# A 14-stage transformer chain in one kernel: inverse roots by logarithm and exponential, squares and an update on GpSimd, and fillers on TensorE between the stages

## The reference

```python
# first block, per sublayer (swiglu, stick-breaking attention or gated recurrence)
h = rmsnorm(x, g) * (1 + scale) + shift
x = x + [0.5 *] (1 + gate) * sublayer(h)
# between the blocks
x = rmsnorm(x, final_norm_g)
# second block, per sublayer (latent attention, convolution, pooling or squared-ReLU MLP)
h = rmsnorm(x, norm_g[i, 0 or 2]) * (1 + scale) + shift
x = x + gate * rmsnorm(sublayer(h), norm_g[i, 1 or 3])
```

## Time and profile before

| what | value |
|---|---|
| timed runs | 2570.82, 2563.72 and 2575.38 us; median 2570.82 us |
| profiled execution, own time | 2580.46 us |
| its span in the profile | 2578.8 us |
| TensorE busy / VectorE / ScalarE / GpSimd | 2358.3 / 1666.9 / 1199.6 / 334.9 us |
| TensorE's mean granted clock | 0.927 of full speed |

### The profile page before, as it was taken

How to read it: one execution, slowest core, us unless ns; L and a number is a source line. 1 busy time by engine, 2 the same in 40 slices (tenths; PEclk the granted TensorE clock), 3 DMA queues, 4 the chain that set the end, 5 groups by cost and what they waited for, 6 DMA issues and landing times.

```text
span 2578.8 us, 43638 instructions
## 1 busy us (share of the span) xinstructions
PE 2358.3 (91%) x17650; PEld 2262.1 (88%) x17650; DVE 1666.9 (65%) x1960; ACT 1199.6 (47%) x1761; POOL 334.9 (13%) x481
## 2 busy tenths in 40 slices
PE   3999999999999958999879999998997899888997
PEld 2999978999999957999848998888996899867997
DVE  6667655667767665767765766855766675654653
ACT  1444445543544464544534543435544554554543
POOL 0111000111111021211000214300201120000210
PEclk6999989999999988999869998998998999888999
DMA  8689763779688723878443775403784477222552
GB/s 309 233 283 315 254 233 102 269 269 326 241 299 293 251 82 124 307 263 296 158 164 104 250 272 183 131 3 121 253 275 133 139 255 249 82 98 66 181 191 70
DMA packets 292525, 523.88 MB, mean 203 GB/s; under 512 B 9318, under 2 KB 184849, under 8 KB 292369
## 3 DMA queue, kind: packets, MB, share of 16 engines
q1 hardware_dynamic: 262417, 358.07, 41.8%
q0 software_dynamic: 29952, 163.59, 17.8%
HBM read 520.57 MB, written 1.05 MB: 202 GB/s over the span
## 4 chain that ended last, share of the span: by engine, by line
PE 87%; DVE 7%; ACT 3%; issue 2%; POOL 0%; ACTq 0%; DVEq 0%; POOLq 0%
PE bk L1210 11%; PE bk L1211 11%; PE bk L1212 11%; PE bk L1118 10%; PE bk L1119 10%; PE bk L1120 10%; PE bk L1261 4%; PE bk L1171 3%; PE bk L1452 2%; PE bk L1191 1%; PE bk L1192 1%; PE bk L1193 1%; DVE inv L1623 1%; DVE mod_acc L1596 1%; PE bk L1316 1%
## 5 line engine op out<-in xcount | busy, mean ns | idle before, releaser
L1577 DVE TENSOR_TENSOR w_lo<-raw,w_hi 128x1024 fp32r<-128x1024 f32 (+5 forms) x720 | 834.2, 1185 | 611.2 <-ACT w_hi L721 609.2
L721 ACT ACTIVATE w_hi<-raw 128x1024 fp32r<-128x1024 f32 (+5 forms) x720 | 684.4, 977 | 737.2 <-PE bk L1120 402.8
L1210 PE MATMUL bk<-a_hi,w_hi 128*128 128x256 f32 x2336 | 668.5, 286 | 4.4 <-DVE a_lo L1643 4.4
L1211 PE MATMUL bk<-a_lo,w_hi 128*128 128x256 f32 x2336 | 667.1, 286 | 0.0
L1212 PE MATMUL bk<-a_hi,w_lo 128*128 128x256 f32 x2336 | 666.7, 285 | 0.0
L1118 PE MATMUL bk<-hid_hi,w_hi 128*128 128x256 f32 x1664 | 465.7, 280 | 0.0
L1120 PE MATMUL bk<-hid_hi,w_lo 128*128 128x256 f32 x1664 | 465.7, 280 | 0.0
L1119 PE MATMUL bk<-hid_lo,w_hi 128*128 128x256 f32 x1664 | 465.7, 280 | 0.0
L1210 PEld LDWEIGHTS bk<-a_hi,w_hi 128*128 128x128 f32 x2336 | 454.3, 194 | 5.1 <-issue 4.5
L1211 PEld LDWEIGHTS bk<-a_lo,w_hi 128*128 128x128 f32 x2336 | 454.2, 194 | 0.0
L1212 PEld LDWEIGHTS bk<-a_hi,w_lo 128*128 128x128 f32 x2336 | 453.9, 194 | 0.0
(11 more groups left out here) (327 smaller groups left out, 3174.8 us busy)
## 6 DMA issues: line engine op xcount, KB each, us to landing
raw<-in_ffn_w SPq DMA_DIRECT2D x128, 1024.0 KB, 5.5
mod_raw<-in_ada_w POOLq DMA_DIRECT2D x128, 768.0 KB, 6.0
raw<-in_ffn_w_gu SPq DMA_DIRECT2D x88, 1024.0 KB, 7.1
mod_raw<-in_mod_w POOLq DMA_DIRECT2D x80, 768.0 KB, 6.7
raw<-in_ffn_w_down SPq DMA_DIRECT2D x40, 1024.0 KB, 6.7
first_mod<-in_mod_w SPq DMA_DIRECT2D x16, 768.0 KB, 6.2
raw<-in_sb_w_qkv SPq DMA_DIRECT2D x12, 1024.0 KB, 5.2
raw<-in_conv_w_pw SPq DMA_DIRECT2D x12, 1024.0 KB, 5.5
```

The lines of the kernel that those rows point to most:

```text
L721: ins = act.activation(o(w_hi[:, p % OPS, :]), r(raw[:, c % RAWS, :]), ACT.Copy)
L1210: pe.matmul(o, wh, a_hi[:, f, :], start=(f == 0), stop=False)
L1211: pe.matmul(o, wh, a_lo[:, f, :], start=False, stop=False)
L1577: ins = dve.tensor_tensor(o(w_lo[:, p % OPS, :]), r(raw[:, c % RAWS, :]), o(w_hi[:, p % OPS, :].bitcast(F32)), ALU.subtract)
```

## The change

1. `root` and `c_root` become `inverse_root`: ScalarE takes Ln to `rms` and, after a wait for itself, Exp with scale -0.5 to `inv`. VectorE's reciprocal goes. The table preloads for the root name the set `natural_log_exp_and_others`, at the places where they were.
2. GpSimd adds the four squares of tiles 0 to 3 to one tile (`first_four`, two operations) in every stage but pool, and `last_piece` sums this one tile instead of four. Tile 4 is no longer summed between output tiles 6 and 7.
3. In the post passages GpSimd updates the last pair of `x` (`last_pair`, two operations). VectorE updates three pairs and passes on GpSimd's signal.
4. The first tile of a stage's input is used in two steps (`first_feature`): its `a_hi` products as soon as `a_hi` is there, the `a_lo` products after it. pool is left as it was.
5. `keep_busy` issues float32 products of `one1` with itself, 128 columns each, whose results nobody reads: 12 ahead of the squares of `x` in the post passages (behind `mod_sum` where there is one), and 8 behind them (there, behind the final norm and in stage 0).
6. In ffn1 VectorE adds half 11 of the second group beside the first output half, ahead of its `residual`. Beside the second output half come halves 12 to 15, and none between the last pieces and `residual`.

```diff
+            def first_four(n):
+                pool.wait_ge(sq_ready, tail_squares[n] + 4)
+                pool.tensor_tensor(sig[:, 0, :, :], sig[:, 0, :, :], sig[:, 1, :, :], ALU.add).then_inc(pool_step, 1)
+                pool.wait_ge(pool_step, k.next("pstep") + 3)
+                pool.tensor_tensor(sig[:, 0, 0, :], sig[:, 0, 0, :], sig[:, 0, 1, :], ALU.add).then_inc(four_ready, 1)
+            def last_pair(n):
+                m = sum(z["kind"] in POST for z in stages[:n])
+                pool.wait_ge(rms_ready, roots_by[n])
+                pool.wait_ge(yg_ready, KD * m + KD)
+                pool.tensor_tensor(tmp[:, 6:8, :], tmp[:, 6:8, :], inv[:, (roots_by[n] - 1) % 2, :].unsqueeze(1).to_broadcast([P, 2, S]),
+                                   ALU.mult).then_inc(pool_step, 1)
+                pool.wait_ge(pool_step, k.next("pstep") + 3)
+                pool.tensor_tensor(x[:, 6:8, :], x[:, 6:8, :], tmp[:, 6:8, :], ALU.add).then_inc(far_ready, 1)
...
@@ in GpSimd's queue, ffn2 (ffn1 likewise, without last_pair)
-                        for r in range(5, KD + 1):
+                        for r in range(5, KD):
                             mod_next(g[0], r)
+                    first_four(st["n"])
+                    if g:
+                        mod_next(g[0], KD)
+                    last_pair(st["n"])
...
@@ at the end of mla and conv first_four and last_pair; of sb and lru first_four; of pool last_pair
...
@@ ScalarE; the other preloads of Sqrt, and Exp in mla, likewise
-                    act.preload_act_table(ACT.Sqrt)
+                    act.preload_act_table_set("natural_log_exp_and_others")
+            def inverse_root(bank, scale):
+                act.wait_ge(mean_done, k.next("mean") + 1)
+                n = k.next("root")
+                act.activation(rms[:, n % 2, :], bank, ACT.Ln, bias=eps_col[:, 0:1], scale=scale).then_inc(log_ready, 1)
+                act.wait_ge(log_ready, n + 1)
+                act.activation(inv[:, n % 2, :], rms[:, n % 2, :], ACT.Exp, scale=-0.5).then_inc(rms_ready, 1)
...
@@ last_piece
-                sums(tail, 0, 4)
+                is_free(pe, tail)
+                pe.wait_ge(four_ready, k.next("tail") + 1)
+                pe.matmul(job_flat(tail, S), ones[:, :], sig[:, 0, 0, :], start=True, stop=False)
+                k.add("sq", 4)
...
-                    if m == 2:
-                        sums(tail, 4, 5)
-                sums(tail, 5, KD)
+                sums(tail, 4, KD)
+            def keep_busy(bank, n):
+                for _ in range(n):
+                    pe.matmul(bank[:, 0:P], one1[:, :], one1[:, :], start=True, stop=True)
+            def first_feature(outs, act_from):
+                pe.wait_ge(ahi_ready, KD * k.next("ahi") + 1)
+                for o, wh, wl in outs:
+                    pe.matmul(o, wh, a_hi[:, 0, :], start=True, stop=False)
+                    pe.matmul(o, wl, a_hi[:, 0, :], start=False, stop=False)
+                pe.wait_ge(act_ready, act_from + 1)
+                for o, wh, wl in outs:
+                    pe.matmul(o, wh, a_lo[:, 0, :], start=False, stop=False)
...
@@ first_feature is called for tile 0 in first_gate_up, gate_up, by_feature and by mla's first columns
...
@@ TensorE, start of a stage, behind mod_sum
+                if after(g) == "post":
+                    keep_busy(job_banks(w)[:, 3, :], 12)
                 if after(g) != "plain":
                     sums(w, 0, KD)
+                    keep_busy(job_banks(w)[:, 3, :], 8)
...
@@ inverse() on VectorE
-                own_wait(own(dve.reciprocal(inv[:, s, :], rms[:, s, :])))
@@ post
-                for q in range(5):
-                    if q < 4:
+                for q in range(4):
+                    if q < 3:
...
+                dve.wait_ge(x_ready, x_count(g) + 6)
+                dve.wait_ge(far_ready, n // KD + 1)
+                dve.sem_inc(x_ready, 2)
@@ ffn1 on VectorE, beside the output halves m = 0, 1
-                            mod_add(st["groups"][1], (5 + 6 * m + u) // 2, (5 + 6 * m + u) % 2)
+                            if u < 6 - 2 * m:
+                                mod_add(st["groups"][1], (5 + 7 * m + u) // 2, (5 + 7 * m + u) % 2)
+                        if m == 0:
+                            mod_add(st["groups"][1], 5, 1)
```

More of the change, by code:

```diff
@@ L361, in build @@
         tail_base = [3 * sum(kd != "pool" for kd in kinds[:n]) for n in range(len(kinds))]
+        tail_squares, sq = [], 0
+        for z in stages:
+            sq += {"plain": 0}.get(after(z["n"]), KD) + {"mla": 5, "conv": KD}.get(z["kind"], 0)
+            tail_squares.append(sq)
+            sq += KD
+        roots_by, roots = [], 0
+        for z in stages:
+            roots += 1 + (after(z["n"]) == "final") + {"mla": 2, "conv": 1}.get(z["kind"], 0)
+            roots_by.append(roots + 1)
+            roots += z["kind"] in POST
         def x_count(n):
@@ L681, in _ @@
                         hid_low(n + 8 + b, 8 + b, b % 2)
-                    for r in range(3, KD + 1):
+                    for r in range(3, KD):
                         mod_next(g + 1, r)
+                    first_four(st["n"])
+                    mod_next(g + 1, KD)
                 elif st["kind"] == "sb":
@@ L1110, in piece, with by_feature @@
                 ins.then_inc(piece_used, 2 if p in double else 1)
-            def by_feature(w):
+            def by_feature(w, act_from=None):
                 def go(wh, wl, xh, xl, first, last):
+                    if first and act_from is not None:
+                        first_feature([(job_banks(w)[:, m, :], wh[:, P * m:P * m + P], wl[:, P * m:P * m + P])
+                                       for m in range(4)], act_from)
+                        return None
                     for m in range(4):
@@ L1186, in first_gate_up @@
                         f = 4 * q + r
+                        if f == 0:
+                            first_feature([(job_banks(w)[:, m, :], *(z[:, (p + m // 2 * 2) % OPS, P * (m % 2):P * (m % 2) + P]
+                                                                     for z in (w_hi, w_lo))) for m in range(4)], act_from)
+                            continue
                         pe.wait_ge(act_ready, act_from + f + 1)
@@ L1204, in gate_up @@
                         f = q % 2 * 4 + r
+                        if act_from is not None and q == 0 and f == 0:
+                            first_feature([(job_banks(w)[:, m, :], *(z[:, p % OPS, P * m:P * m + P] for z in (w_hi, w_lo)))
+                                           for m in range(2)], act_from)
+                            continue
                         if act_from is not None and q < 2:
@@ L1336, in _ @@
                             for r in range(2):
+                                if n == 0 and q + r == 0:
+                                    first_feature([(job_banks(w)[:, m, :], w_hi[:, p % OPS, a:a + P], w_lo[:, p % OPS, a:a + P])
+                                                   for m, a in enumerate(starts)], nq)
+                                    continue
                                 if n == 0:
```

33 lines of the change are left out of this document (18 added, 15 removed).

## The result

The changed kernel takes 2557.93 us (median of 18 runs), the kernel before 2573.46 us beside it (18 runs, the three shown ahead of the prediction among them). The ratio is 0.994, with a 95% interval of 0.9928 to 0.9952: 0.6% or about 15.5 us faster, where 40.6 were forecast. The profiled execution has a span of 2558.9 us against 2578.8: 19.9 less.

The account below looks back on a forecast made before the run. TensorE is busy 91% of the span, so gains lie in passages where it waits or runs at a reduced clock. 17.0 + 0.6 + 7.6 + 0.5 + 14.9 = 40.6 us off the median 2570.8 gives 2530 us, range 2512 to 2561.

Parts of the forecast that it names:

- the price of the fillers behind `mod_sum`: Post passages behind 6, 7, 9, 11: the 12 fillers lie on the path and cost 2.8 us.
- the stall in ffn1: Fifth piece of ffn1's second output half: TensorE stalls for half 11's landing time less 4.9 us, taken as 1.2 us.
- dead fillers: Rival: fillers don't raise the clock and run at the low level, 5.1 and 3.4 us; gain 10.4, 2560 us; chance 0.17.
- Root: Every norm: `inv` 1.0 us after the last `ones` product, not 2.34; each root on the path gains 1.3 us.
- a rival for all roots: Ln and Exp load a table each: 1.28 us on some 15 roots on the path, 2550 us; chance 0.04.
- First products: Passages that wait for the norm: first product 2.05 us earlier, root included; only 1.3 for pool.
- Tails: Stage ends: `first_four` hidden on GpSimd, fewer `ones` rows; 1.0 us in each of six post stages, 1.6 in the last, 7.6 together.
- Post passages without `mod_sum`: Behind stages 8, 10, 12: 2.25 us between the norms, 2.05 first product, 1.35 clock; 5.65 a passage, 17.0 together.
- `last_pair` waits for VectorE's six: Post passages without `mod_sum`: GpSimd's two operations start after VectorE's six and end 7.2 us after the first norm's last `ones` product.
- Post passages with `mod_sum`: Behind 6, 7, 9, 11: loses 3.35, wins 2.05 and 2.2, net 0.9 three times; -2.05 behind stage 9; 0.6 together.
- Clock behind the norm: After the first product: fillers win back clock, 1.35 us a passage without `mod_sum`, 0.6 with it.
- GpSimd beside VectorE: Rival: GpSimd runs at the same time as VectorE, `x` ready 1.8 us earlier in three passages, 2525 us; chance 0.12.

Follow-up runs that it names:

- sqrt_back: v_pair with square root, its table and VectorE's reciprocal in place of logarithm and exponential; 2561.43 us, ratio 0.9957 to the kernel before.
- v_pair: Changed kernel with the last pair of `x` updated on VectorE again instead of GpSimd; 2546.25 us, ratio 0.9887 to the kernel before.
- b_pre_four: combo_b with 4 fillers ahead of every `mod_sum` that stands in a passage, except in the first; 2527.89 us, ratio 0.9814 to the kernel before.
- no_fill: Changed kernel with neither the 12 nor the 8 fillers at the start of a stage; 2549.76 us, ratio 0.9893 to the kernel before.
- no12_mod: Changed kernel without the 12 fillers in the four post passages that have a `mod_sum`; 2552.79 us, ratio 0.9902 to the kernel before.
- combo_b: Changed kernel without the 12 fillers at `mod_sum`, last pair on VectorE, ffn1 halves in old order but half 15 behind `residual`; 2535.15 us, ratio 0.9855.
- b_mixed: b_pre_four with one filler behind every fourth column of `mod_sum`; 2538.55 us, ratio 0.9869 to the kernel before.

## Why the prediction was half right

The direction was right, the amount 2.6 times too large (40.6 against 15.5). Three steps failed: the order of `last_pair` and VectorE, the price of the fillers behind `mod_sum`, and the stall in ffn1. Together they are 26 us short of the forecast; smaller terms and bodies that came out better give some 6 back (by the 19.9 us of the profiled executions). The measured 2558 lies in the stated range, but only at the end that was set for the dead fillers. Step by step:

- **Root**: right but for one. Forecast `inv` at M + 1.0 and 1.3 us a root; measured 0.92 and 1.34 (sqrt_back), and no table load between Ln and Exp in 27 of 28 roots. In stage 0, where no preload of the common set stands ahead of the root, there is one, which the forecast had as a rival for all roots ("that may hold for the preload alone"):

```profile
68.85 0.47 ACT L792 ACTIVATE rms<-bk,eps_col 128x256 f32<-128x256 f32 x1 [12.23 <-PE bk L1229]
69.35 1.28 ACT L794 ACT_TABLE_LOAD   x1
70.64 0.42 ACT L794 ACTIVATE inv<-rms 128x256 f32<-128x256 f32 x1
```

  The load for the function behind it (71.07), which the reciprocal had covered, now stands ahead of `a_hi` too. The first product of stage 0 comes 4.60 us after the root and not 4.11.
- **First products**: right where there is nothing else on ScalarE. The steps for them add up to 17.7 us (six times 2.05, 1.3 for pool, 2.05 behind stage 5, 2.0 behind lru), measured 16.8. That the sums agree so well is in part luck. The six, pool and stage 5 gave 12.1, 1.3 and 1.9, but lru only 0.8: two pieces (1.99 us) stand behind the root on ScalarE, and `a_hi` waits for them. Stage 0 lost 0.5, and the plain passages with `mod_sum`, of which nothing was forecast, gave 1.2.
- **Tails**: right. Without the end of the kernel 21.8 us were forecast (four ffn1 at 2.9, 1.7, 1.5, and 7.0 for the post stages), measured 21.7. GpSimd was not starved: the two operations of `first_four` took 1.29 to 2.59 us and 0.73 to 2.13 us, and TensorE never waited for it.
- **Post passages without `mod_sum`**: wrong. Three times 2.25 us were forecast between the roots and -0.3 measured on average (0.1, -0.6 and -0.5). The failing step is "`last_pair` waits for VectorE's six". I read the 7.33 us of the earlier trace rows as an order, VectorE first. It only showed that the two don't overlap. They alternate, the first pair comes 2.1 us later than with VectorE alone (root + 5.0 against 2.9), TensorE idles 3.22 us behind the fillers, and the squares then run at a mean clock of 0.70. v_pair took both away. For pool I had overlooked ScalarE's queue. The forecast's 0.9 us for the last two `ones` products was also the price of the high level, four rows at 0.24 (8 rows in 1.89), and not that of the 0.42 named beside it, which gives 1.7.
- **Post passages with `mod_sum`**: wrong, the largest miss. Forecast 8.6 us lost between the roots (3.35 each, less 1.6 in three), measured 18.9. The price of the fillers, 2.8 us, came from the high level, "because TensorE would not be idle before them". But `mod_sum`'s own rows had run into the low level before, as the 8.4 us of the earlier trace rows against 5.5 of the earlier trace rows said. The low price was the right one, 5.33 us; two rows at twice 0.115 are 0.46 a filler and 5.5 for 12, not the 5.1 of the forecast. And `mod_sum` itself got 1.4 us longer on average in these four (from 6.1 to 7.5 us, first to last start). The forecast had seen that ScalarE's longer root delays it, and priced that at 0.55 us alone; sqrt_back and b_pre_four show that the idle time also goes with a longer `mod_sum`.
- **ffn1**: the formula, landing time less 4.9 us, held (7.75 less 4.9 is 2.85, measured 2.6). The landing was taken at the median of all loads, 6.2, where three of four took some 7.6; and a stall's second price, 1 to 2 us at a low clock behind it, was missing from the sum. 13.1 us were lost in the four bodies, 4.8 forecast.
- **Clock behind the norm**: better than forecast. The four ffn2 bodies are 2.1 us shorter on average, not 1.35 or 0.6, but no_fill shows that most of it does not come from the fillers.

The rival of dead fillers (2560) came nearest the time, 2558, and that is luck. Only its low price where `mod_sum` stands is right, and even there the clock is up behind the fillers (the squares take 3.7 us with them and 6.1 without, no12_mod). Without `mod_sum` the fillers did run at the high level. Its sum was also 2 us short: it leaves out stage 5's 1.7 of the tail, and the passage into pool is 4.3 by its own terms (0.5 + 5.1 - 1.3), not 4.6. "GpSimd beside VectorE" was excluded too, since in every passage an operation of the one is longer by what the other does meanwhile.

## What to carry to other kernels

Moving part of a chain to an idle engine helps only if it does not cost the engine that holds the chain's *first* part: ask who gets the shared resource first, not only when the last part is ready. A step that gets shorter on one path can get longer on another: the new root is sooner there for VectorE, but ScalarE is busy for 0.5 us more, and what waits for ScalarE behind it starts later. Price an inserted instruction at the clock which the instructions just ahead of it have, and a stall at its length plus what the clock costs behind it. Where a transfer is wanted earlier, move the work that is not urgent behind the urgent one instead (half 15 behind the residual): this kept the whole gain without the stall.

## What the runs showed of the hardware

- GpSimd and VectorE, both with operations of two inputs from on-chip memory, take turns: a multiplication of 128 x 512 took 1.70 to 1.78 us in all eight passages of the changed kernel on GpSimd (a subtraction of that size took 1.27 alone), and VectorE's addition 1.75 in place of 0.68. The Trainium skill ("GPSIMD Engine Reference", section "1. Specifications") says that both share their interfaces to that memory and contend when VectorE has two inputs there; the trace agrees, and adds that neither is preferred in this pattern. In the earlier trace rows, with VectorE's 18 operations back to back, GpSimd got no turn; what makes the difference was not tried.
- `mod_sum`, 48 rows of one column, took from 5.2 to 8.9 us from its first to its last start in the post passages of the kernels that have nothing between its columns. The clock falls to 0.50 at some point in or after it, and the point differs between passages of one run. The idle time ahead of it has a part in this. Two pairs of kernels differ in it, 0.62 against 0.11 us (v_pair and sqrt_back, by the root) and 0.62 against none (combo_b and b_pre_four, by four fillers), and in all eight comparisons `mod_sum` is shorter with less idle time, by 0.04 to 2.6 us. But it does not decide it alone: b_pre_four still has 7.1 us behind stage 6 and 5.2 behind stage 9. What else sets it stays open, and fillers inside it (b_mixed) did not hold it up.
- The attention of the second mla ran at 0.50 for 30 us in b_pre_four and at 0.69 and 1.00 in combo_b. The window rows of TensorE, of b_pre_four and then of combo_b:

```profile
2245.00:2260.00 15.00, 15.00 (x46) 0.50 0.00 1
2260.00:2275.00 15.00, 15.00 (x52) 0.50 0.00 0
```

```profile
2245.00:2260.00 15.00, 15.00 (x64) 0.69 0.00 0
2260.00:2275.00 15.00, 10.62 (x62) 1.00 0.00 1
```

  The body of that stage was 138.2 us in the one and 130.0 in the other, though nothing in it differs. Over the 13 changed kernels it took 129.7 to 132 us or 136.6 to 138.2, so up to eight us of scatter between profiled executions come from this stage. An edit worth less than 0.3% was therefore judged here by its own stretch of the trace.
